# Order of small products, the end of a convolution in chunks with idle products, and early sums, evictions and table loads in a two-block decoder layer

## The reference

```python
# first block
h = rmsnorm(x, ln1); hq, hk, hv, hr, ha, hatt, hgate = split(h @ w_in)
log_a = log_sigmoid(ha @ w_a2 + b_a) / 16
o = gla_mixer(hq, hk, hv, log_a)        # 4 heads, chunks of 64 tokens, a state from chunk to chunk
y_gla = (rms_of_head(o) * gla_gn * silu(hr)) @ w_o_gla
o_att = three groups of dilated causal windows, merged by softmax of their lse; y_att = o_att @ w_o_attn
x = x + (sigmoid(g_gla) * y_gla + sigmoid(g_att) * y_att) @ w_out
x = x + square(relu(rmsnorm(x, ln2) @ w_mlp1)) @ w_mlp2
x = rmsnorm(x + sigmoid(rmsnorm(x, ln3) @ w_pg) * (p @ w_pp), ln_f)
# second block: two layers; layer 0 mixes with a convolution, layer 1 with latent attention (mla)
for i in range(2):
    h = h + 0.5 * swiglu_ffn(rmsnorm(h), ffn1_w1[i], ffn1_w3[i], ffn1_w2[i])
    m = rmsnorm(h, mix_norm[i])
    if i == 0:   # u = a * sigmoid(b) of m @ w_pw1; causal depthwise convolution over 31 tokens;
        h = h + silu(rmsnorm(conv(u), g_norm)) @ w_pw2
    else:        # 8 heads, 128 + 64 (rope) features in each score, mask by chunks of 64 tokens
        h = h + mla(m, positions)
    h = h + 0.5 * swiglu_ffn(rmsnorm(h), ffn2_w1[i], ffn2_w3[i], ffn2_w2[i])
return rmsnorm(h, final_norm)
```

## Time and profile before

| | |
|---|---|
| median of 3 runs | 1523.23 us (1521.88 to 1523.64) |
| the profiled execution's own time | 1522.38 us |
| its span, first to last instruction | 1520.7 us |
| its mean granted TensorE clock | 0.995 |
| PE, PEld, DVE, ACT, POOL busy | 1489.8, 1329.1, 1140.4, 747.8, 39.5 us |
| read from HBM | 257.73 MB, 170 GB/s over the span |

### The profile page before, as it was taken

The page is one execution under the profiler, slowest core; times in us unless marked ns, Lnnn a source line. Parts: engine busy times, 40 slices in busy tenths (PEclk is TensorE's granted clock), DMA queues, the critical chain, the costliest instruction groups (busy, mean ns, idle before and its releaser), DMA issues.

```text
span 1520.7 us, 25169 instructions
## 1 busy us (share of the span) xinstructions
PE 1489.8 (98%) x9754; PEld 1329.1 (87%) x9754; DVE 1140.4 (75%) x1517; ACT 747.8 (49%) x1008; POOL 39.5 (3%) x77
## 2 busy tenths in 40 slices
PE   8999999999999999999998999999999999999997
PEld 6878899998888988888986888899888997888887
DVE  6867866789865688787876877678776697887754
ACT  5635456544443375444544545445544444555443
POOL 1000000200000000000121000000000000000000
PEclk9999999999999999999999999999999999999999
DMA  7636665566656466646632666567665654466553
GB/s 233 174 111 180 185 181 155 153 187 185 193 181 193 156 178 192 185 137 186 213 113 71 191 182 192 159 189 211 190 189 156 198 157 146 121 184 191 165 170 111
DMA packets 268919, 260.12 MB, mean 171 GB/s; under 512 B 15702, under 2 KB 267172, under 8 KB 268826
## 3 DMA queue, kind: packets, MB, share of 16 engines
q1 hardware_dynamic: 267120, 256.41, 56.9%
q0 software_dynamic: 1072, 1.98, 0.5%
q10 hardware_dynamic: 634, 0.44, 0.1%
HBM read 257.73 MB, written 1.07 MB: 170 GB/s over the span
## 4 chain that ended last, share of the span: by engine, by line
PE 61%; DVE 2%; ACT 1%; issue 1%; DVEq 0%; ACTq 0%
PE ps L598 30%; PE ps L604 15%; PE ps L639 12%; PE misc L841 2%; PE misc L792 1%; PE misc L673 0%; PE misc L669 0%; DVE wsplit L1235 0%; PE ps L816 0%; PE misc L795 0%; ACT sq L1010 0%; DVE x L1414 0%; DVE plain L1297 0%; DVE acc L1452 0%; DVE work L1412 0%
## 5 line engine op out<-in xcount | busy, mean ns | idle before, releaser
L1235 DVE TENSOR_TENSOR wsplit<-raw,wsplit 128x1024 fp32r<-128x1024 f32 (+2 forms) x532 | 585.3, 1129 | 110.8 <-ACT wsplit L970 99.9
L970 ACT CAST wsplit<-raw 128x1024 fp32r<-128x1024 f32 (+2 forms) x532 | 494.4, 968 | 177.2 <-DMA raw<-in_ffn_w_dram 89.8
L598 PE MATMUL ps<-xa,wsplit 128*128 128x512 f32 x1552 | 398.7, 393 | 0.3 <-PE misc L694 0.3
L598 PEld LDWEIGHTS ps<-xa,wsplit 128*128 128x128 f32 x1552 | 285.2, 188 | 59.6 <-DVE val L1285 1.4
L598 PE MATMUL ps<-parts,wsplit 128*128 128x512 f32 x1068 | 292.0, 397 | 6.8 <-DVE parts L1264 5.5
L598 PEld LDWEIGHTS ps<-parts,wsplit 128*128 128x128 f32 x1068 | 198.3, 190 | 48.2 <-issue 5.9
L998 ACT COPY lohalf<-ps 128x512 f32<-128x512 f32 x152 | 89.0, 585 | 297.3 <-PE ps L598 240.9
L604 PE MATMUL ps<-xa,wsplit 128*128 128x256 f32 x1552 | 232.6, 282 | 0.0
L1285 DVE TENSOR_TENSOR val<-ps,lohalf 128x512 f32<-128x512 f32 x152 | 105.1, 691 | 150.6 <-ACT lohalf L998 150.0
L604 PEld LDWEIGHTS ps<-xa,wsplit 128*128 128x128 f32 x1552 | 211.6, 191 | 6.7
L604 PE MATMUL ps<-parts,wsplit 128*128 128x256 f32 x1068 | 179.9, 283 | 0.0
(11 more groups left out here) (263 smaller groups left out, 999.2 us busy)
## 6 DMA issues: line engine op xcount, KB each, us to landing
raw<-in_ffn_w_dram SPq DMA_DIRECT2D x176, 512.0 KB, 3.8
raw<-in_w_in_dram SPq DMA_DIRECT2D x76, 512.0 KB, 3.7
raw<-in_ffn_w_dram SPq DMA_DIRECT2D x96, 384.0 KB, 3.1
raw<-in_w_mlp_dram SPq DMA_DIRECT2D x64, 512.0 KB, 3.6
raw<-in_conv_w_pw_dram SPq DMA_DIRECT2D x24, 512.0 KB, 3.9
raw<-in_ffn_w_dram SPq DMA_DIRECT2D x32, 256.0 KB, 3.1
raw<-in_w_o_gla_dram SPq DMA_DIRECT2D x8, 512.0 KB, 3.6
raw<-in_w_out_dram SPq DMA_DIRECT2D x8, 512.0 KB, 3.5
```

Of the source, the lines that this page charges most:

```text
L598: return mm(ps[:, bank, c, :], still, both.rearrange("p h t -> p (h t)"), start=p.k0[j] + kk == 0, stop=end, skip_group_check=True)
L970: nc.scalar.copy(wsplit[:, slot, 0:kn, 0, 0:p.width], raw[:, slot, 0:kn, 1, 0:p.width]).then_inc(hi_done, 1)
L1235: TT(wsplit[:, slot, 0:kn, 1, 0:p.width], raw[:, slot, 0:kn, 1, 0:p.width], wsplit[:, slot, 0:kn, 0, 0:p.width].bitcast(F32), ALU.subtract ...
```

## The change

- `upd0`: for each head, chunk 0 and then chunk 1. `o`: first the eight products on 128 columns, then all those on 64 columns. `attend`, masked: both halves' 128-row products, both 64-row ones, both masks.
- The convolution's last chunk goes to a bank of `ps` (`conv_last`), each chunk of pair 3 signals by itself, ACT squares them one by one, and the sum waits for each half alone. Pairs 0 and 3 are normalised chunk by chunk, and the first pair goes through SiLU and the split chunk by chunk. Eight products whose result nobody reads stand behind the sum, ahead of `pw2`.
- `ffn1_up0`: the sums at groups 1 and 18 stand ahead of the group's blocks. `w_pg1`, `w_pg2`: DVE's `evacuate` stands ahead of the second block.
- ACT runs a one-element activation (`load_table`) of Sqrt at the start (behind a wait for `ident_ready`), of Sigmoid in `w_pg0` behind the root of the gains, and of Sqrt ahead of the last group's eviction.

```diff
+        conv_last = ps[:, 1 - by["pw1"].group0 % 2, 0, 0:T]
+        def conv_out(i, c):
+            return conv_last if (i, c) == (3, 1) else misc[:, i, c * T:(c + 1) * T]
...
-                else:
-                    pe.wait_ge(squared, q + 4)
                 for c in range(1 if early else 2):
+                    if not early and c == 0:
+                        pe.wait_ge(half_squared, 1)
+                    if not early and c == 1:
+                        pe.wait_ge(squared, q + 4)
...
-                    for n in range(2) if k == "upd0" else (2,):
-                        if n == 2:
-                            dv_did(pe, "st0")
-                        t, r = n // 2, (n % 2) * GLA_CHUNK
-                        for h in range(GLA_H):
+                    chunks = (0, 1) if k == "upd0" else (2,)
+                    if k == "upd2":
+                        dv_did(pe, "st0")
+                    for h in range(GLA_H):
+                        for n in chunks:
+                            t, r = n // 2, (n % 2) * GLA_CHUNK
...
-                               plain[:, 8 + 2 * h + t, :], start=True, stop=False, skip_group_check=True)
+                               plain[:, 8 + 2 * h + t, :], start=(h % 2 == 0), stop=False, skip_group_check=True)
+                    for t in range(NT):
+                        for h in range(GLA_H):
+                            at = t * D + h * GLA_DV
...
+                    if masked:
+                        places = [o0[:, 0:P], o1[:, 0:T]]
+                        for n, (q, k) in enumerate(qk(0)):
+                            for t in range(NT):
+                                mm(places[t], q[:, t * P:(t + 1) * P], k[:, 0:(t + 1) * P], start=(n == 0 and t == 0),
+                                   stop=False, skip_group_check=True)
+                        for t in range(NT):
+                            last = mm(places[t][:, t * P:(t + 1) * P], mask[:, 0, :], mask[:, 1, :], start=False,
+                                      stop=True, skip_group_check=True)
...
-                            last = mm(misc[32 * q:32 * q + 32, i, c * T:(c + 1) * T], conv_w(2 * i + c)[:, m, q, :],
+                            last = mm(conv_out(i, c)[32 * q:32 * q + 32, :], conv_w(2 * i + c)[:, m, q, :],
...
-                last.then_inc(s_pe, 1)
+                    if c == 1 or i == 3:
+                        last.then_inc(s_pe, 1)
...
                     conv_sum(False)
+                    for _ in range(8):
+                        mm(ps[:, 1, 1, 0:T], ones[:, :], cos[:, :], start=True, stop=True, skip_group_check=True)
...
+            def load_table(func):
+                act_fn(idle[0:1, :], ident[0:1, 0:1], func)
...
+            act.wait_ge(ident_ready, 1)
+            load_table(ACT.Sqrt)
...
+                            load_table(ACT.Sigmoid)
...
+                        if p.evac[0] == "out" and g == 3:
+                            load_table(ACT.Sqrt)
                         evacuate(p, g, None, 0)
...
-                    for c in (2, 3):
-                        square_pair("conv", c, misc[:, c, :].rearrange("p (k t) -> p k t", k=2))
+                    square_pair("conv", 2, misc[:, 2, :].rearrange("p (k t) -> p k t", k=2))
+                    q = pairs["conv"][0] + 3
+                    act.wait_ge(summed, q - 1)
+                    pe_did(act, "conv3a")
+                    act_fn(sq[:, q % 2, 0, :], conv_out(3, 0), ACT.Square).then_inc(half_squared, 1)
+                    pe_did(act, "conv3")
+                    act_fn(sq[:, q % 2, 1, :], conv_out(3, 1), ACT.Square).then_inc(squared, 1)
...
                     for i in range(4):
-                        dv_did(act, f"convn{i}")
                         for c in (2 * i, 2 * i + 1):
+                            dv_did(act, "convn0a" if c == 0 else f"convn{i}")
...
-                        last.then_inc(s_ac, 1)
-                        settle()
+                            if c == 0 or c % 2:
+                                last.then_inc(s_ac, 1)
+                                settle()
...
+                        if p.name == "ffn1_up0" and g in (1, 18):
+                            for c in (2,) if g == 1 else (3, 4):
+                                add_squares("ffn1_up0", c)
                         for j in range(len(p.kns)):
+                            if p.name in ("w_pg1", "w_pg2") and j == 1:
+                                evacuate(p, g, None, 0)
                             ahead(p, g, j, None)
...
-                        if p.name == "ffn1_up0" and g in (1, 18):
-                            for c in (2,) if g == 1 else (3, 4):
-                                add_squares("ffn1_up0", c)
...
-                        evacuate(p, g, None, 0)
+                        if p.name not in ("w_pg1", "w_pg2"):
+                            evacuate(p, g, None, 0)
...
-                        if i < 4:
+                        if i in (0, 3):
+                            for c in range(2):
+                                ins = TT(unit(2 * i + c), conv_out(i, c), rstd[:, :], ALU.mult)
+                                if i == 0 and c == 0:
+                                    done("convn0a", ins)
+                            done(f"convn{i}", ins)
+                        elif i < 4:
...
-                        if i:
+                        if i == 1:
+                            for c, name in enumerate(("conv0a", "conv0")):
+                                ac_did(v, name)
+                                split(parts[:, 16 + c:17 + c, :, :], units(c, 1), 1)
+                        elif i:
```

More of the change, by code:

```diff
@@ L215, in program @@
         stat = sb("stat", [P, 24])
+        idle = sb("idle", [1, 1])
         gain_rows = logit[0:GAIN_N, 0:P]
@@ L449, in program @@
         conv_w_ready = sem("conv_w_ready")
+        half_squared = sem("half_squared")
         conv_w_dve = sem("conv_w_dve")
@@ L493, in program @@
                    + [n for h in range(3) for n in (f"att{h}.pT", f"att{h}.pv", f"att{h + 1}.qk0", f"att{h + 1}.qk")]
-                   + ["att3.pT", "att3.pv", "pT", "tapsT", "conv0", "conv1", "conv2", "conv3", "rope_k", "rope_q0", "rope_q1", "ckv.tokT"]
+                   + ["att3.pT", "att3.pv", "pT", "tapsT", "conv0", "conv1", "conv2", "conv3a", "conv3", "rope_k", "rope_q0", "rope_q1", "ckv.tokT"]
                    + heads(("qk", 0), ("pT", 2), ("pv", 3)) + ["ffn2_up1.tokT", "xtok0", "xtok1"])
@@ L498, in program @@
                    + [f"att{h}.{s}" for h in range(ATT_H) for s in ("max", "norm", "o")]
-                   + ["ple_in", "lnf_gain", "taps", "lnf0", "lnf1", "lnf2", "lnf3", "glu0", "glu1", "glu2", "glu3"] + [f"convn{i}" for i in range(4)]
+                   + ["ple_in", "lnf_gain", "taps", "lnf0", "lnf1", "lnf2", "lnf3", "glu0", "glu1", "glu2", "glu3"] + ["convn0a"] + [f"convn{i}" for i in range(4)]
                    + ["rope_k", "rope_q0", "rope_q1"]
@@ L503, in program @@
                    + [f"att{h}.{s}" for h in range(ATT_H) for s in ("exp", "pT")]
-                   + ["lnf_gain"] + ["conv0", "conv1", "conv2", "conv3"] + heads(("exp", 0), ("pT", 2))
+                   + ["lnf_gain"] + ["conv0a", "conv0", "conv1", "conv2", "conv3"] + heads(("exp", 0), ("pT", 2))
                    + ["xtok0", "xtok1", "outroot"])
@@ L757, in gla_step @@
                                       start=True, stop=True, skip_group_check=True)
-                        last.then_inc(s_pe, 1)
+                            if h == GLA_H - 1:
+                                last.then_inc(s_pe, 1)
                 if k == "o":
@@ L786, in attend @@
                     o0, o1 = logit_banks(ng, par)
-                    for t in range(NT):
+                    if masked:
[7 more added lines that the diff above has]
+                                      stop=True, skip_group_check=True)
+                    for t in range(0 if masked else NT):
                         for g in range(ng):
                             o = o1[:, g * T:(g + 1) * T] if t else o0[:, g * P:(g + 1) * P]
[L790 to L793, removed]
-                            if masked:
-                                last = mm(o[:, t * P:(t + 1) * P], mask[:, 0, :], mask[:, 1, :], start=False, stop=True,
-                                          skip_group_check=True)
-                        if ng > 1 and t == 0:
+                            q, k = qk(g)[0]
+                            last = mm(o, q[:, t * P:(t + 1) * P], k[:, 0:(t + 1) * P], start=True, stop=True,
+                                      skip_group_check=True)
+                        if t == 0:
                             last.then_inc(s_pe, 1)
```

## The result

The changed kernel takes 1509.16 us in the median of 4 runs (1508.31 to 1509.24) against 1523.24 for the one before (1521.88 to 1523.64, 4 runs): ratio 0.9909, interval 0.9898 to 0.992, 14.1 us faster. The prediction said 1508.8, and a range of 1506.0 to 1513.5. The profiled execution took 1508.31 us, with a span of 1506.6; the prediction had 1508.5 and 1506.8.

What follows compares the result with a forecast made beforehand. TensorE was taken as the bound, its products covering 1489.8 of 1520.7 us. Terms summing to 13.9 us took the profiled execution from 1522.38 to 1508.5 us; the forecast median was 1508.8, range 1506.0 to 1513.5.

Steps and rivals of the forecast that it cites:

- The recurrence: `o` and `upd0`: fewer changes of shape in `o` save 2.4 us, row halves side by side in `upd0` 0.9 us.
- The heads: Masked heads of the second attention: three changes of shape instead of six, 0.46 us less per head, 3.7 us in all.
- loses part of its lead and gets it back in head 3: VectorE is full in the first three heads, so TensorE loses some lead there but recovers it in head 3.
- The gates: `w_pg` and `w_pp` products: early sigmoid table and early taking of `w_pg1` and `w_pg2` remove a TensorE wait, 1.4 us.
- The sum and the clock behind it: `ffn1_up0`, group 18: sums first save 2.2 us of waiting, and the half clock behind that wait goes, 1.7 us.
- The convolution: Convolution's end: half squares and chunks start the first product earlier, idle products keep the idle stretch short; 0.8 us.
- then VectorE is the limit: Behind the convolution, VectorE's pairs, 1.9 us apart, set the pace; the first group ends at 830.6 against 831.4.
- The tail: Kernel's end: the last root's table load, issued a group earlier, is hidden and the root comes sooner; 0.8 us.

Runs made afterwards that it cites:

- sum late and filled: Changed kernel with group 18's sums in `ffn1_up0` behind its two blocks again and five idle products ahead of the sum's product: 1511.25 us.
- the tables: Changed kernel with two more table loads moved ahead, Sqrt between the convolution's half squares and Exp in `ukv_nope`: 1509.19 us.
- the cast on ScalarE: Changed kernel with the high halves of the convolution's `parts` written by ScalarE instead of VectorE: 1508.54 us.
- the late sum's run: Changed kernel with the sums of group 18 of `ffn1_up0` behind the group's two blocks again: 1512.01 us.

## Why the prediction was right

**The recurrence** (2.4 and 0.9 predicted, 2.4 and 1.0 measured). The price of a change of shape, 0.17 us by dividing the excess over streamed columns by the number of changes, held when 14 of the 16 were taken away, and the row halves ran side by side.

**The heads** (3.7 predicted, 2.97 measured): this term was mis-sized. The head itself shrank by 0.49 as placed; the step that failed is "loses part of its lead and gets it back in head 3". In head 3 TensorE waits for VectorE's `plain` (L1349, 0.18 us, and stops and starts around it), which keeps 0.44 of that head's 0.49. What is given back there isn't recovered. That makes 8 x 0.49 - 0.44 = 3.5 us, and the experiments show it: four traces in which the clock stayed full (sum late and filled, twice the idle products, the tables, the cast on ScalarE) win 3.50 to 3.54 us in this stretch, a fifth (`w_pg3` early) 3.07, having lost 0.4 ahead of the heads. The first three heads with what lies between take 9.94 to 9.96 us against 11.44 before. In the kernel after's one trace another 0.53 is missing, and ScalarE's timeline shows where:

```profile
1260.35 1.05 ACT L997 CAST wsplit<-raw 128x1024 fp32r<-128x1024 f32 x1 [3.88 <-DMA raw<-in_mla_w_o_dram]
1261.42 1.28 ACT L1117 ACT_TABLE_LOAD   x1
1262.71 0.37 ACT L1117 ACTIVATE logit<-misc,stat 128x128 f32<-128x128 f32 x1
```

A block of `w_o` landed late, and head 0's exponentials stand behind its rounding in ScalarE's queue. In the kernel with twice the idle products the same rounding starts at 1258.03, after 1.96 us. So this is one execution's transfer. Why it landed late isn't settled.

**The gates** (1.4 predicted, 1.8 measured). `w_pp1` starts without a wait, `w_pg2` after 0.68, and `ffn1_up0` after 1.38 where 1.6 was expected. Here the trace of the kernel before was enough to say that part of what is won comes back as a longer wait.

**The sum and the clock behind it** (2.2 and 1.7 predicted, 2.25 and 1.6 measured). The first is shown by the late sum's run. The second is right for the two profiled executions compared, and a matter of chance otherwise.

**The convolution** (0.8 predicted, 1.1 measured). Mechanism as predicted: 16 idle records in 3.62 us, then 1.65 us of waiting, first product 5.1 us behind the sum, VectorE's pairs the limit after that. The idle products were counted at no cost, and they have none; that they bring nothing either was in the same sentence ("then VectorE is the limit") and only the run without them made it plain.

**The tail** (0.8 predicted, 0.9 measured). VectorE's product, the reduce and the root of the kernel after:

```profile
1500.06 0.69 DVE L1424 TENSOR_TENSOR plain<-plain 128x512 f32<-128x512 f32 x1 [0.16 <-DVE plain L1418]
1500.79 0.16 DVE L1777 TENSOR_REDUCE half_tok<-sum_tok 128x2 f32<-128x8 f32 x1
1500.98 0.29 ACT L1238 ACTIVATE root_tok<-half_tok,consts 128x2 f32<-128x2 f32 x1 [0.53 <-DVE half_tok L1777]
```

The root follows the reduce at once; no load stands between them, as one did in the earlier trace rows.

**The sum.** The heads' term is 0.73 too large and the others together are 0.9 too small, 0.2 at the start among it that nothing predicted; so the total is good partly because errors cancel. It is luck, too, that the clock stayed full in the heads' tail in the execution compared: it fell there in seven of thirteen traces and cost 0.7 to 1.1 us, a fall that the prediction didn't foresee. The profiled execution is 0.85 us under the median (1508.31, 1509.16), exactly as before. The prediction had let 0.55 of that distance go with the clock lost at the two waits; it stayed, so its cause is another, and the varying start and the fall in the heads' tail are candidates; the runs around the median have no trace.

## What to carry to other kernels

Where small products of several shapes alternate, count the changes of shape in the timeline, price one from the excess over the streamed columns, and issue equal shapes together: the kernel with nothing but that had 6.0 of the 13.9 us that lie behind the start. For every wait that an edit removes, follow the waiting engine's queue to the next thing that is late: at the gates and in head 3 part of the gain came back there, and at the convolution's end the clock trick was worth nothing because another engine's chain set the end. Compare profiled executions by the shift of one and the same instruction, stretch by stretch, since single executions start differently by more than most edits are worth.

## What the runs showed of the hardware

**The start varies, and the clock column doesn't show it.** The first group's 12 records of 256 columns in two kernels, and the window around them in the second:

```profile
11.02 1.78 PE L647 MATMUL ps<-xa,wsplit 128*128 128x256 f32 x12
```

```profile
11.77 3.12 PE L647 MATMUL ps<-xa,wsplit 128*128 128x256 f32 x12
```

```profile
10.00:16.00 6.00, 5.71 (x20) 5.12 (x21) 5.66 (x12) 3.68 (x6) 0.00 (x0) 1.00 1.10 348
```

The first is the kernel after, the second the one with `w_pg3` taken early, whose code is the same up to there. Its records stand 0.21 us apart instead of 0.12, up to 16 us. The 1.00 of the window isn't a measured full clock: the trace's own list of granted clocks begins late, and the column counts what lies before its first entry as full. That entry, at full clock, begins at 9.2 us in the kernel after and at 16.1 us in this one. In the trace of `w_pg1` and `w_pg2` taken late it begins at 13.3 us, and in the first group there the spacing goes from 0.21 to 0.12 us between 13.2 and 13.4 us. And 0.21 us is the spacing of such records where half clock is recorded (824.35 to 824.57 in the kernel before). So these starts run at half clock until the first entry. In the fourteen traces it begins at 8.0 to 9.2 us in eight, at 13.3 in three and at 16.1 to 16.6 in three; the later ones cost 1.3 us and 2.6 to 2.9 us. The code up to there is all but the same in the fourteen, so this is a matter of the execution; what decides it isn't shown.

**Whether the clock falls behind a short wait differs from one execution to the next.** Behind a wait of 2.3 us ahead of the sum it fell in two traces and not in a third. In the heads' tail it fell for 3.4 us in seven of the thirteen traces since the change or its order was in, and cost some 0.7 to 1.1 us each time. All thirteen have a wait of 1.41 us between small products there, and those in which the clock is still full behind it one of 0.36 more. The kernel before has a wait of 1.4 us there too, and its one trace shows no fall; whether the new order makes the fall likelier is open. Behind the 5.1 and 5.5 us at the convolution's end it fell in all three traces that have such a wait.
